# A long convolution of a mixer layer by discrete Fourier sums: transforms of even and odd tokens apart, with 256 frequencies instead of 512

## The reference, cut to what matters

```
def hyena_mixer(u, sw, sb, filt, skip):
    u = short_conv(u, sw, sb)
    x0, x1, v = jnp.split(u, 3, axis=-1)
    z = (v * x1).astype(F32)
    L = z.shape[1]
    Z = jnp.fft.rfft(z, n=2 * L, axis=1)
    Hf = jnp.fft.rfft(filt, n=2 * L, axis=0)
    y = jnp.fft.irfft(Z * Hf[None], n=2 * L, axis=1)[:, :L]
    y = y + z * skip.astype(F32)
    return y.astype(u.dtype) * x0
```

## Time and profile before

| | before |
|---|---|
| median of 3 runs | 2196.08 us (2191.68 to 2196.54) |
| the profiled execution | 2197.11 us |
| its span | 2195.3 us |
| mean granted clock of PE | 0.973 |
| PE busy | 2046.6 us (93%) |
| DVE busy | 709.4 us (32%) |
| ACT busy | 544.8 us (25%) |
| POOL busy | 106.5 us (5%) |

### The profile page before, as it was taken

How to read it: one execution, slowest core, us unless ns; L and a number is a source line. 1 busy time by engine, 2 the same in 40 slices (tenths; PEclk the granted TensorE clock), 3 DMA queues, 4 the chain that set the end, 5 groups by cost and what they waited for, 6 DMA issues and landing times.

```text
span 2195.3 us, 22621 instructions
## 1 busy us (share of the span) xinstructions
PE 2046.6 (93%) x9298; PEld 1268.0 (58%) x9298; DVE 709.4 (32%) x1023; ACT 544.8 (25%) x832; POOL 106.5 (5%) x119
## 2 busy tenths in 40 slices
PE   8999999989899888989897989998999999999998
PEld 6766843333333333333332577787777788887886
DVE  6735430101010010101010554622566543435324
ACT  5135220000010000000000463233343342224225
POOL 3420000000000000000000000231000000000000
PEclk9999999999999999999999999899999999999999
DMA  9510589999999999999999322110113213222331
GB/s 264 150 49 3 220 347 428 427 428 428 429 428 428 428 429 429 428 429 429 428 428 428 138 111 77 39 39 26 66 64 115 96 58 115 76 103 103 110 134 58
DMA packets 48454, 516.53 MB, mean 235 GB/s; under 512 B 5872, under 2 KB 6000, under 8 KB 12800
## 3 DMA queue, kind: packets, MB, share of 16 engines
q1 hardware_dynamic: 45808, 508.39, 56.9%
q0 software_dynamic: 2576, 7.14, 1.5%
HBM read 509.18 MB, written 6.29 MB: 235 GB/s over the span
## 4 chain that ended last, share of the span: by engine, by line
PE 74%; DMA 19%; DVE 3%; ACT 2%; issue 1%; POOL 0%; SPq 0%; DVEq 0%; ACTq 0%
DMA arena<-in_w_gu_dram 19%; PE bank L2319 12%; PE bank L2341 6%; PE bank L892 4%; PE bank L891 4%; PE bank L893 4%; PE bank L568 3%; PE bank L569 3%; PE bank L570 3%; PE bank L2257 2%; PE bank L923 2%; PE bank L925 2%; PE bank L924 2%; PE bank L2285 2%; PE bank L1960 2%; PE bank L1954 2%
## 5 line engine op out<-in xcount | busy, mean ns | idle before, releaser
L2319 PE MATMUL bank<-arena 128*64 128x512 f32 x2048 | 479.7, 624 | 81.4 <-DMA arena<-in_w_gu_dram 80.4
L2319 PEld LDWEIGHTS bank<-arena 128*64 128x64 f32 x2048 | 161.8, 143 | 369.2 <-issue 368.2
L2759 DVE TENSOR_TENSOR arena<-arena,bank 128x256 f32<-128x256 f32 x64 | 27.0, 421 | 686.0 <-ACT arena L2989 686.0
L2341 PE MATMUL bank<-arena 128*64 128x512 f32 x1024 | 232.3, 594 | 0.7 <-ACT arena L2993 0.6
L2989 ACT ACTIVATE arena<-bank 128x256 f32<-128x256 f32 x64 | 24.5, 383 | 549.2 <-PE bank L2319 549.2
L2341 PEld LDWEIGHTS bank<-arena 128*64 128x64 f32 x1024 | 76.4, 137 | 141.1 <-issue 141.1
L892 PE MATMUL bank<-input_rest,weight_rounded 128*128 128x512 f32 x352 | 140.3, 399 | 0.0
L891 PE MATMUL bank<-input_rounded,weight_rest 128*128 128x512 f32 x352 | 140.2, 398 | 0.0
L893 PE MATMUL bank<-input_rounded,weight_rounded 128*128 128x512 f32 x352 | 138.2, 392 | 0.0
L568 PE MATMUL bank<-input_rounded,weight_rest 128*128 128x512 f32 x312 | 131.1, 420 | 4.3 <-DVE weight_rest L980 4.3
L569 PE MATMUL bank<-mix_rest,unit_rounded 128*128 128x512 f32 x312 | 126.9, 407 | 0.0
(11 more groups left out here) (492 smaller groups left out, 2961.6 us busy)
## 6 DMA issues: line engine op xcount, KB each, us to landing
arena<-in_w_gu_dram SPq DMA_DIRECT2D x126, 2048.0 KB, 28.7
arena<-in_w_d_dram SPq DMA_DIRECT2D x63, 2048.0 KB, 25.6
arena<-in_wpack_dram SPq DMA_DIRECT2D x83, 1024.0 KB, 5.0
arena<-in_w_gu_dram SPq DMA_DIRECT2D x3, 1024.0 KB, 6.6
arena<-in_xT_dram SPq DMA_DIRECT2D x4, 512.0 KB, 6.6
arena<-in_x_dram SPq DMA_DIRECT2D x2, 1024.0 KB, 13.3
arena<-in_x_dram SPq DMA_DIRECT2D x1, 2048.0 KB, 8.6
ple_kept<-arena SPq DMA_DIRECT2D x8, 256.0 KB, 5.3
```

The lines of the kernel that those rows point to most:

```text
L2319: last = mm(ab[64 * x:64 * x + 64, :], xsT[:, k, 64 * x:64 * x + 64], w[x][k], start=k == 0, stop=k == KD - 1)
L2341: last = mm(bank[4 + n][64 * x:64 * x + 64, :], hidT[c % 2][:, P * t + 64 * x:P * t + 64 * x + 64], w[:, x, t, 512 * n:512 * n + 512], sta ...
```

## The change

The matrix of 512 tokens by 512 frequencies has a symmetry: frequency 512 - k gives the same sums over even tokens as frequency k and the opposite sums over odd tokens (for the sines the other way round). The changed kernel sorts the tokens by parity, transforms even and odd tokens apart for frequencies 0 to 255 only, and gets both halves of the spectrum as sum and difference.

- PE: eight calls `fourier(n)` with two tiles of tokens each, where eight calls had four; each call's result is read by itself. The alternating sum over the filter takes half the matmuls. `inverse(m, odd)` has four calls with matmuls of 256 columns, where they had 512; all four now stand at u = 5 and 6.
- ACT: four copies of 128x512 (`odd_copied`) and four scaled copies of 128x512 (`scaled_filter`, twice) take the place of eight copies of 128x256. `out_weight_rounded(1)` goes from u = 3 to u = 4, `out_weight_rounded(0)` from u = 4 to u = 5.
- DVE: `cosine_sums`, `sine_sums`, `spectrum_products` and `spectrum`, each for two tiles of frequencies, take the place of `spectrum` for four; `turn_sines` is gone. The products and the first two combinations are 128x512 instructions. `filtered(0)` and `out_weight_rest(1, 1)` go from before `attend(6)` to before `attend(7)`.
- POOL: four additions of 128x256 (`even_made`).
- The trigonometric tables come in one DMA of 1.75 MB instead of two with 2 MB together. The filter's taps and the turned z are read with a step of two tokens, and `filtered` writes so.

```diff
+            def fourier(n):
+                f, part, odd = n // 4, n // 2 % 2, n % 2 == 0
+                free = {3: ("rs_made", 1), 4: ("spec_made", 1), 5: ("rs_made", 2), 6: ("spec_made", 2), 7: ("rs_made", 5)}
+                if n in free:
+                    name, v = free[n]
+                    pe.wait_ge(S(name), nth(name, v))
+                b = fbank[n % 3]
+                w = (cos_of, sin_of)[part][odd]
+                for i in range(2):
+                    last = mm(b[:, :], w[:, i, P * f:P * f + P], zqp[:, 2 * odd + i, 256 * part:256 * part + 512],
+                              start=i == 0, stop=i == 1)
...
+            def inverse(m, odd):
+                b = fbank[2 - 2 * m][:, 256 * odd:256 * odd + 256]
+                if m == 0 and odd == 0:
+                    pe.wait_ge(S("ywf_made"), 2)
+                    pe.wait_ge(S("even_made"), nth("even_made", 2))
+                for f in range(2):
+                    mm(b, ywf[:, f, 256 * odd + P * m:256 * odd + P * m + P], inv_cos[odd][:, f, :], start=f == 0, stop=False)
...
-            fourier(0, 0)
-            fourier(0, 1)
+            for n in range(3):
+                fourier(n)
             for u in range(8):
                 if u < 7:
                     scores(u + 1)
                 if u < 3:
-                    fourier(u + 1, 0)
+                    fourier((3, 5, 7)[u])
...
-                if 3 <= u < 7:
-                    inverse((u - 3) // 2, range(2 * ((u - 3) % 2), 2 * ((u - 3) % 2) + 2))
+                if u in (5, 6):
+                    inverse(u - 5, 0)
+                    inverse(u - 5, 1)
                 turn_weights(u)
-                if u < 3:
-                    fourier(u + 1, 1)
+                if u < 2:
+                    fourier((4, 6)[u])
...
+            def spectrum_products(f):
+                dve.wait_ge(S("rs_made"), nth("rs_made", 4 * f + 4))
+                dve.wait_ge(S("spec_made"), nth("spec_made", 3 * f + 2))
+                own.wait()
+                own(tt(out=codd[f], in0=zc, in1=fc, op=ALU.mult))
+                own(tt(out=sodd[f], in0=zs, in1=fc, op=ALU.mult))
+                own.wait()
+                if f == 0:
+                    own(tt(out=fc[0:1, 0:256], in0=zs[0:1, 256:512], in1=fs[0:1, 0:256], op=ALU.mult))
+                    own(tt(out=fc[0:1, 256:512], in0=zs[0:1, 0:256], in1=fs[0:1, 256:512], op=ALU.mult))
+                    own.wait()
+                own(tt(out=zc, in0=zc, in1=fs, op=ALU.mult))
+                own(tt(out=zs, in0=zs, in1=fs, op=ALU.mult))
+                own.wait()
...
             attend(0)
+            cosine_sums(0)
+            attend(1)
+            sine_sums(0)
+            spectrum_products(0)
+            attend(2)
             spectrum(0)
-            attend(1)
-            spectrum(1)
-            attend(2)
             dve.wait_ge(S("pooled_made"), 2)
             weigh(0)
-            spectrum(2)
             attend(3)
-            spectrum(3)
-            turn_sines()
+            cosine_sums(1)
             attend(4)
+            sine_sums(1)
+            spectrum_products(1)
+            spectrum(1)
             weigh(1)
-            out_weight_rest(1, 0)
             attend(5)
             channel_variance(1)
-            filtered(0)
-            out_weight_rest(1, 1)
+            out_weight_rest(1, 0)
             attend(6)
             channel_root(1, 1)
             channel_scale(1, 1)
+            filtered(0)
+            out_weight_rest(1, 1)
             weigh(2)
             attend(7)
...
+            def odd_copied(f, part):
+                n = 4 * f + 2 * part
+                act.wait_ge(S("four_filled"), nth("four_filled", n + 1))
+                fn((codd, sodd)[part][f], fbank[n % 3][:, :], ACT.Copy).then_inc(S("rs_made"), 1)
+
             def scaled_filter(f):
...
+                act.wait_ge(S("spec_made"), nth("spec_made", 3 * f + 1))
+                fn(csum[:, 0, :], csum[:, 0, :], ACT.Copy, scale=col("wk", f)).then_inc(S("rs_made"), 1)
+                act.wait_ge(S("spec_made"), nth("spec_made", 3 * f + 2))
+                fn(ssum[:, 1, :], ssum[:, 1, :], ACT.Copy, scale=1.0 / L).then_inc(S("rs_made"), 1)
...
-                if u < 3:
-                    scaled_filter(u + 1)
-                if u == 3:
-                    act.wait_ge(S("ywf_made"), NT)
+                if u in (0, 3):
+                    scaled_filter(u // 3)
+                if u in (1, 2):
+                    odd_copied(1, u - 1)
+                if u == 4:
+                    act.wait_ge(S("ywf_made"), 2)
                     out_weight_rounded(1)
...
```

More of the change, by code:

```diff
@@ L2074, in weighted @@
                 last.then_inc(S("pv_filled"), 1)
[L2076 to L2099, removed]
+            def fourier(n):
[9 more added lines that the diff above has]
+                              start=i == 0, stop=i == 1)
+                    if n == 3 and i == 0:
+                        for t in range(2):
+                            mm(b[0:1, 256:512], col("alt2"), filt[:, t, 256:512], start=False, stop=False)
+                last.then_inc(S("four_filled"), 1)
@@ new lines, in inverse @@
+            def inverse(m, odd):
[3 more added lines that the diff above has]
+                    pe.wait_ge(S("even_made"), nth("even_made", 2))
+                for f in range(2):
+                    mm(b, ywf[:, f, 256 * odd + P * m:256 * odd + P * m + P], inv_cos[odd][:, f, :], start=f == 0, stop=False)
+                    last = mm(b, ywf[:, f, 512 + 256 * odd + P * m:512 + 256 * odd + P * m + P], inv_sin[odd][:, f, :],
+                              start=False, stop=f == 1)
+                if odd:
@@ L2526, in _, with by_sign @@
                 .then_inc(S("pq_made"), 1)
-            def spectrum(f):
[L2529 to L2532, removed]
+            def by_sign(v, o):
+                return v.rearrange("p a (b c) -> p a b c", c=256)[:, :, o, :]
@@ new lines, in cosine_sums @@
+            def cosine_sums(f):
+                dve.wait_ge(S("four_filled"), nth("four_filled", 4 * f + 2))
+                dve.wait_ge(S("rs_made"), nth("rs_made", 4 * f + 1))
+                e = fbank[(4 * f + 1) % 3].rearrange("p (a c) -> p a c", c=256)
+                o = codd[f].rearrange("p (a c) -> p a c", c=256)
+                own(tt(out=by_sign(csum, 0), in0=e, in1=o, op=ALU.add))
+                tt(out=by_sign(csum, 1), in0=e, in1=o, op=ALU.subtract).then_inc(S("spec_made"), 1)
@@ L2533, in spectrum @@
+            def spectrum(f):
+                if f == 0:
+                    stt(out=codd[0], in0=zs, scalar=col("nkeep"), in1=codd[0], op0=ALU.mult, op1=ALU.add)\
+                        .then_inc(S("spec_made"), 1)
+                else:
+                    tt(out=codd[f], in0=codd[f], in1=zs, op=ALU.subtract).then_inc(S("spec_made"), 1)
+                own(tt(out=sodd[f], in0=sodd[f], in1=zc, op=ALU.add))
                 own.wait()
-                n = own(tt(out=ywf[:, f, 0:256], in0=pr[0], in1=pr[1], op=ALU.subtract))
+                plus, minus = sodd[f][:, 0:256], sodd[f][:, 256:512]
+                own(tt(out=ywf[:, f, 512:768], in0=plus, in1=minus, op=ALU.subtract))
@@ L2535, in spectrum @@
                 if f == 0:
+                    own(tt(out=ywf[:, f, 768:1024], in0=plus, in1=minus, op=ALU.add))
                     own.wait()
[L2537 to L2540, removed]
+                    own(tt(out=ywf[0:1, 0, 512:768], in0=zs[0:1, 256:512], in1=zs[0:1, 0:256], op=ALU.subtract))
@@ L3025, in tables @@
     ang = 2 * np.pi * ((k[:, None] * k[None, :]) % (2 * L)) / (2 * L)
[L3026 to L3027 removed]
+    sines, cosines = np.sin(ang), np.cos(ang)
+    halves = [cosines[0::2, :256], cosines[1::2, :256], sines[0::2, :256], sines[1::2, :256]]
+    for w in halves[2:]:
+        w[:, 0] = (-1.0) ** k[:256]
+    halves += [halves[1].T, halves[2].T, halves[3].T]
+    four = np.concatenate([w.reshape(2, P, 256).transpose(1, 0, 2).reshape(P, 512) for w in halves], 1).astype(f)
     consts = np.concatenate([np.eye(P), np.ones((P, P)), np.triu(np.ones((P, P))), np.triu(np.ones((P, P)), 1)], 1)
@@ L3122, in lay_out @@
     put("freq", a["hy_f_freq"])
-    put("wk", c["wk"])
+    put("wk", c["wk"][:256])
+    put("keep", np.arange(P) > 0)
+    put("nkeep", -1.0 * (np.arange(P) > 0))
     put("negt", c["negt"])
@@ L3145, in lay_out @@
     )
-    for n in ("cosm", "sinm", "consts", "invc", "mask", "pos", "deltas", "iota", "blk"):
+    for n in ("four", "consts", "invc", "mask", "pos", "deltas", "iota", "blk"):
         d[n] = c[n]
```

81 lines of the change are left out of this document (46 added, 35 removed), and 1 row of the table at.

## The result

The changed kernel takes 2200.98 us (median of 7 runs, 2198.49 to 2202.80); the kernel before takes 2192.48 us (7 runs on the same chips, 2191.68 to 2196.54). The ratio is 1.0032, with a 95% interval of 1.0021 to 1.0044. By the ratio it is slower by 7 us (4.6 to 9.6), by the two medians by 8.5, though TensorE has less to do.

A forecast was written before the change was run, and what follows sets the result against it. The mixer stage sets the start of the expert weights' stream; PE bounds its first half, an 8.2 us ring through PE, DVE and ACT every step. Queues -4.2, slow clock +7.8 and +2.5 give +6.1 us: 2202 us, range 2191 to 2208.

The forecast's parts named there:

- PE bound only in the first half: Mixer stage: PE's work alone bounds its first 44.3 us; the following 34.1 us are bound by something else.
- the ring's floor of 8.2 us: Mixer stage: scores, attend, exps, copies and weighted through PE, DVE, ACT and back; no step u under 8.2 us.
- DVE's three delays: DVE's queue: attend(2), attend(5) and attend(7) stand behind spectrum or filter work, late by 3.1, 4.2 and 2.5 us.
- They are not on this path: POOL's additions: start with spectrum(1), wanted by the inverse 9 us later, so put at no cost.
- The clock in the stage: PE at 1.2 GHz from u = 1's end to the inverse: 7.8 us for six slow pieces, 2.5 in u = 5.
- Behind the stage: After weighted(6): all that follows keeps its order and its distances, so no time won or lost there.
- the upper bound: All six pieces, u = 5 whole, weighted(6) and the output product's first twelve matmuls at slow clock: +11.2 us.
- a rival with one chance in ten: Output product: the slow clock lasts into it, +11 us, 2207 us; chance 0.10.
- the wait of 0.76 us: Kernel before, ahead of weighted(6): PE's wait taken as bringing the half clock at 216.55 us, for 3.4 us.
- That the clock holds: Rival, mixer stage: remaining transforms keep PE at 2.4 GHz through the gaps; -4.2 us, 2192 us; chance 0.2.
- Smaller waits of DVE: Rival, mixer stage: ACT and DVE interleave better, the three delays go; -14.0 us, 2182 us; chance 0.08.
- PE's work counted in full: Rival, mixer stage: all the PE time removed is won; -21.7 us, 2174 us; chance 0.02.

The follow-up runs named there:

- e5_order_fill: e4_all with attend(5), weigh(1) and filtered(0) earlier in DVE's queue, ACT's work moved to suit, and filler matmuls in u = 1 to 4; 2181.2 us, ratio 0.9942.
- e4_all: Changed kernel with unread filler matmuls in PE's waits (none in u = 1), attend(2) ahead of spectrum_products(0), and POOL's additions after DVE's spectrum; 2186.8 us, ratio 0.9965.
- e8_before_fill: Kernel before the change, with two unread filler matmuls of 256 columns in u = 6 behind the transposes; 2193.0 us, ratio 0.9998.
- e3_pool: Changed kernel with POOL's additions started only when DVE is through with the tile's spectrum; 2202.1 us, ratio 1.0035.
- e2_attend: Changed kernel with attend(2) ahead of spectrum_products(0) in DVE's queue and spectrum(0) behind attend(3); 2199.5 us, ratio 1.0022.
- e6_order: e5_order_fill with every filler matmul left out; 2188.1 us, ratio 0.9976.

## Why the prediction was right

The forecast was 2202 us, slower; measured were 2201.0 us and a ratio clear of one. Most steps came out as written, and the sum was helped by two errors that cancel. That 2202 lies within 1 us of the median is luck on top: it stands on the three runs' 2196.08 us for the kernel before, and seven runs gave 2192.48. On that base +6.1 us would be 2198.6.

- **PE bound only in the first half; the ring's floor of 8.2 us.** Right. `scores(1)` starts 8.13 us after `scores(0)` (forecast 8.0), and the fastest kernel's steps settle at 8.2.
- **DVE's three delays.** Forecast 3.1, 4.2 and 2.5 us; measured, against `scores` at full clock, 2.7 (155.46 less 152.72), 3.9 and 2.6. Their causes were the ones named, L2924's copy for the first two. e5_order_fill, without them, has a stage 5.2 us shorter than e4_all, which has the last two. The second delay holds 0.9 us that I had not seen, from POOL's additions beside DVE's. "They are not on this path" was wrong: in the changed kernel because they slow DVE's, and in the fastest kernels because the first inverse waits for them.
- **The clock in the stage: +10.3 forecast.** `weighted(1)`, `scores(3)`, `weighted(4)` and `scores(6)` were slow, at 1.7 and 0.95 us each as sized. `weighted(2)` and `scores(4)` were not: the clock was back by then, behind `fourier(7)`, 3.78 us long at half clock. That is 2.6 us too much in the sum. The step u = 5 took 10.2 us; that is 2.0 over the ring with 0.9 of it in `scores(6)`, so 1.1 in place of 2.5. The stage had 82.7 us where 209.5 - 134.26 + 10.3 = 85.5 was forecast.
- **Behind the stage: 0 forecast, +3.3 measured.** I had written that all that follows keeps its distances, and had put the slow clock in the output product into the upper bound and into a rival with one chance in ten. It was what happened in the changed kernel's trace, without `weighted(6)` being slow. The slow stretch begins behind the wait of 3.33 us and `weighted(6)`, and has the transposes, the sums and the first twelve matmuls of the product in it; six fillers in that wait took 4.8 us off.
- **What lets the clock fall.** I gave the wait of 0.76 us in the kernel before as the reason of its slow stretch. e8_before_fill has the stretch without that wait, so this reading of the earlier trace rows was wrong, and the price taken from longer waits held nevertheless.
- **The sum.** +6.1 us forecast, 6.5 us by the two traces, 7 us by the ratio.
- **The rivals.** That the clock holds, at 2192, is what the filled kernel came near to, at 2189.8: 3.7 us under the kernel before by the ratio, where 4.2 were forecast. The split is another one: the trace has 1.4 us less in the stage and 1.6 less behind it, where all 4.2 were put in the stage. The two kernels differ only in the fillers, and in the traces by PE's clock. Smaller waits of DVE, at 2182, is the kernel with the new order and the fillers, 2181.2; its stage has 67.5 us, where 65.4 was forecast, and 1.6 us come from behind it. PE's work counted in full would have been 2174; no kernel came near it.
- Strided reads cost next to nothing: the weight load of a z transpose takes 207 ns instead of 141 (L2048 and L2036, medians of eight), but its matmul 283 ns instead of 273. What is not settled is why each run's clock falls where it does; in three traces of nearly the same work (changed, e3_pool, e2_attend) it fell in u = 1, u = 1 and u = 2, and `weighted(6)` was slow in the last two.

## What to carry to other kernels

When a change takes work from the busiest engine, look first for the ring through the other engines that bounds a step once that work is gone: here 21.7 us of matmuls were worth 4 us at most, until the queues of DVE and ACT were put in a new order (12 us with fillers, 5 without). Then ask what the freed time does to the busy engine's clock: waits of 2.5 to 4 us among short matmuls made the kernel slower than it had been, and matmuls that nobody reads, put into those waits, gave 11 us back. Where an instruction waits for another engine's late copy, put whatever the ring needs next ahead of it in the queue.

## What the runs showed of the hardware

- TensorE at 1.2 GHz isn't a matter of long waits alone. In e8_before_fill the clock fell at 216.5 us with no wait of PE in the 10.8 us before; at their end stood 64-column matmuls, transposes and one-column matmuls, in which the profile counts PE as busy. In e6_order it fell behind waits of 0.67 and 2.47 us. But `weighted(6)`, transposes and one-column sums, here behind a wait of 0.74 us, were followed by full clock in e5_order_fill and e6_order (1.00 from 201.5 to 217 us in the first), so neither the wait nor these pieces decide it alone, and the runs leave open what does. Matmuls of few columns double at half clock as well: sixteen of 64 columns 1.97 to 3.68 us, sixteen of one column 1.84 to 3.41.
- POOL's additions of 128x256 slow DVE's that run beside them and read two SBUF operands, from 0.42 us to 0.83 and 0.94, and are slowed themselves: L1920 and L1921 took 1.11 and 0.91 us beside DVE, and 0.72 each in e3_pool, where they run behind DVE's. The trace of the changed kernel, POOL:

```profile
184.76 1.11 POOL L1920 TENSOR_TENSOR arena<-arena 128x256 f32<-128x256 f32 x1 [24.11 <-DVE arena L2589]
185.83 0.91 POOL L1921 TENSOR_TENSOR arena<-arena 128x256 f32<-128x256 f32 x1
```

  The Trainium skill, "GPSIMD Engine Reference", section "1. Specifications", has it that GpSimd shares its SBUF interfaces with VectorE, and that they collide when a VectorE instruction has two SBUF inputs. The traces agree.
